# Prompt attention: the order of scores, weights' turns and value products on TensorE, and of exponents and copies on ScalarE

## The reference, cut to what matters

```python
o_c = p_c @ v_c                                   # compressed branch, 31 block keys
s_s = q @ k_s - slope * dist; p_s = softmax(s_s)  # "selected" branch (at 512 tokens all blocks are kept)
s_w = q @ k_w - slope * dist; p_w = softmax(s_w)  # window branch
o   = gate_c * o_c + gate_s * (p_s @ v_s) + gate_w * (p_w @ v_w)
```

## Time and profile before

| | |
|---|---|
| median of three runs | 1815.88 us |
| the profiled execution's own time | 1821.45 us |
| its span in the profile | 1819.7 us |
| share of the span busy: PE, DVE, ACT, POOL | 94%, 44%, 29%, 18% |
| the prompt attention stage, first maxima to last values | about 847.9 to 1030.6 us of the span |

### The profile page before, as it was taken

The page is one execution under the profiler, slowest core; times in us unless marked ns, Lnnn a source line. Parts: engine busy times, 40 slices in busy tenths (PEclk is TensorE's granted clock), DMA queues, the critical chain, the costliest instruction groups (busy, mean ns, idle before and its releaser), DMA issues. The chain is left out here.

```text
span 1819.7 us, 26521 instructions
## 1 busy us (share of the span) xinstructions
PE 1715.9 (94%) x9999; PEld 1139.1 (63%) x9999; DVE 794.3 (44%) x1937; ACT 520.8 (29%) x1247; POOL 336.4 (18%) x352
## 2 busy tenths in 40 slices
PE   8999999999999999998888899999998998999987
PEld 6587777877877878887665655575443443444332
DVE  1154664664664410566888552662222222222216
ACT  2234234233233221565667342111111110111110
POOL 0010211211111120222454550001111111111100
PEclk9999999999999999997999999989999999999998
DMA  8071221231232243452000673987999999999987
GB/s 246 1 225 49 71 75 49 60 86 49 60 77 56 48 113 110 118 163 65 1 1 1 232 229 133 386 331 296 400 419 421 420 420 420 421 419 420 419 344 318
DMA packets 168543, 371.70 MB, mean 204 GB/s; under 512 B 36903, under 2 KB 114719, under 8 KB 143584
## 3 DMA queue, kind: packets, MB, share of 16 engines
q1 hardware_dynamic: 148208, 308.69, 46.1%
q0 software_dynamic: 19728, 60.06, 9.4%
q10 hardware_dynamic: 480, 1.25, 0.2%
HBM read 337.75 MB, written 48.15 MB: 212 GB/s over the span
## 5 line engine op out<-in xcount | busy, mean ns | idle before, releaser
L860 PE MATMUL bank<-xT,arena 128*128 128x272 f32 x1440 | 368.1, 399 | 0.0
L860 PEld LDWEIGHTS bank<-xT,arena 128*128 128x128 f32 x1440 | 259.8, 190 | 62.3 <-issue 16.3
L2893 PE MATMUL bank<-arena,kvt 128*64 128x512 f32 (+1 forms) x816 | 258.5, 619 | 18.7 <-issue 17.8
L2893 PEld LDWEIGHTS bank<-arena,kvt 128*64 128x64 f32 (+1 forms) x816 | 88.1, 150 | 152.4 <-issue 152.4
L2990 PE MATMUL bank<-arena,kvt 128*64 128x512 f32 (+1 forms) x408 | 127.8, 598 | 2.3 <-issue 2.1
L3316 DVE SCALAR_TENSOR_TENSOR kvt<-kvt,arena,bank 128x256 f32<-128x256 f32 x37 | 17.8, 481 | 238.6 <-ACT kvt L3098 238.6
L1297 POOL TENSOR_TENSOR arena<-arena 128x512 f32<-128x512 f32 x40 | 46.4, 1160 | 381.3 <-DVE arena L1388 256.9
L2893 PE MATMUL bank<-xT,kvt 128*64 128x512 f32 (+1 forms) x208 | 95.4, 613 | 9.4 <-issue 9.4
L2730 POOL DMA_INDIRECT hT<-x_rows,rows_i x37 | 37.6, 1017 | 356.4 <-DVE rows_i L3251 334.3
L3098 ACT ACTIVATE kvt<-bank 128x256 f32<-128x256 f32 x37 | 14.2, 385 | 276.4 <-PE bank L2893 276.4
L3331 DVE COPY arena<-bank 128x512 f32<-128x512 f32 x37 | 25.6, 692 | 140.3 <-PE bank L2990 140.3
(11 more groups left out here) (519 smaller groups left out, 2971.8 us busy)
## 6 DMA issues: line engine op xcount, KB each, us to landing
arena<-in_w_exp_gate SPq DMA_DIRECT2D x51, 1024.0 KB, 21.4
arena<-in_w_exp_up SPq DMA_DIRECT2D x51, 1024.0 KB, 25.1
arena<-in_w_exp_down SPq DMA_DIRECT2D x51, 1024.0 KB, 23.5
arena<-in_w_in SPq DMA_DIRECT2D x48, 512.0 KB, 5.5
kvt<-in_w_exp_down SPq DMA_DIRECT2D x13, 1024.0 KB, 23.8
xT<-in_w_exp_gate SPq DMA_DIRECT2D x13, 1024.0 KB, 20.4
xT<-in_w_exp_up SPq DMA_DIRECT2D x13, 1024.0 KB, 25.1
y_rows<-arena SPq DMA_DIRECT2D x1, 12800.0 KB, 40.2
```

Of the source, the lines that this page charges most:

```text
L860: last = mm(banks[2 * (i % 2) + half][:, 0:HALF], wh[blk % RING][:, k, :], xT[:, k, half * HALF:(half + 1) * HALF], start=(k == 0), stop=( ...
L2893: last = mm(banks[2 + 4 * (t % 2)][cols, :], xgT[:, k, cols], ewgu[i % EBUF][:, :, k], start=(k == 0), stop=(k == KD - 1))
```

## The change

Three loops' orders change; no arithmetic is added or left out. On PE, `scores(i+3)` stands between the two parts of `turn_weights(i)` (the first part has t//2+1 fills: 1, 1, 2 and 2 for t = 0 to 3), except in rounds before 0 and in the four rounds with `cmp_scores`, where it still comes first. `values` is cut by branch into two halves, one in round 2u+2 and one in round 2u+3. On ACT, `exps(i+2)` no longer goes ahead of the copies of step i: its first branch follows the copies of the first part, its second branch the last copy.

```diff
--- before.py
+++ after.py
@@ -338,6 +338,12 @@
             if i >= 0:
                 P_FILL[i] = len(FILLS)
                 FILLS += ["a"] * (STEPS[i][0] + 1)
+
+        CMP_STEPS = [cmp_at(t) for t in range(4)]
+
+        def turned_first(i):
+
+            return STEPS[i][0] // 2 + 1
 
         def unit_gates(t, j):
 
@@ -1797,26 +1803,28 @@
                             last = tr(banks[4 + f % 2][:, (2 * br + g) * P:(2 * br + g + 1) * P], sc_p[i % 4][:, g, br, k * P:k * P + P], ident[:, :])
                     last.then_inc(tp_banked, 1)
 
-            def values(u):
+            def values(u, half):
 
                 t, j0 = STEPS[2 * u]
                 m = j0 // 2
-                if u >= 2:
-                    pe.wait_ge(mg_ready, u - 1)
-                last_fill = P_FILL[2 * u + 1] + t
-                pe.wait_ge(tp_saved_a, FILLS[0:last_fill + 1].count("a"))
                 out = banks[6 + u % 2]
-                for i in range(4):
-                    par, g = divmod(i, 2)
-                    mm(out[par * HD:par * HD + HD, g * P:g * P + P], vc_p[:, i], PcT[t % 2][:, m], start=(g == 0), stop=False)
-                for br in range(2):
+                if half == 0:
+                    if u >= 2:
+                        pe.wait_ge(mg_ready, u - 1)
+                    last_fill = P_FILL[2 * u + 1] + t
+                    pe.wait_ge(tp_saved_a, FILLS[0:last_fill + 1].count("a"))
+                    for i in range(4):
+                        par, g = divmod(i, 2)
+                        mm(out[par * HD:par * HD + HD, g * P:g * P + P], vc_p[:, i], PcT[t % 2][:, m], start=(g == 0), stop=False)
+                for br in (half,):
                     for k in range(t + 1):
                         for g in range(KVH):
                             c0 = (br + 1) * 256 + P + g * HD
                             for par in range(2):
                                 last = mm(out[par * HD:par * HD + HD, g * P:g * P + P], kvt[:, k, c0:c0 + HD],
                                           PT[u % 2][:, br, k, par, g * P:g * P + P], start=False, stop=(br == 1 and k == t and g == 1))
-                last.then_inc(pv_banked, 1)
+                if half == 1:
+                    last.then_inc(pv_banked, 1)
 
             halves = [slice(0, 64), slice(64, 128)]
 
@@ -1872,7 +1880,8 @@
                 last.then_inc(new_banked, 1)
 
             for i in range(-3, NSTEP + 1):
-                if i + 3 < NSTEP:
+                ahead = i < 0 or i in CMP_STEPS
+                if ahead:
                     scores(i + 3)
                 for t in range(4):
                     if cmp_at(t) == i:
@@ -1886,11 +1895,16 @@
                     turn_weights(i, 2, 4)
                     group_sums()
                 elif 0 <= i < NSTEP:
-                    turn_weights(i)
+                    turn_weights(i, 0, turned_first(i))
+                    if i + 3 < NSTEP and not ahead:
+                        scores(i + 3)
+                    turn_weights(i, turned_first(i))
                 if i == NSTEP - 2:
                     compressed_scores()
-                if i >= 2 and i % 2 == 0:
-                    values(i // 2 - 1)
+                if i >= 2:
+                    values(i // 2 - 1, i % 2)
+                if i == NSTEP:
+                    values(i // 2 - 1, 1)
 
 
             def turn_keys(x):
@@ -2064,20 +2078,24 @@
                 actv(gkv[0:HD, :, 0:NCMP_S], hsum[0:HD, :, 0:NCMP_S], ACT.Gelu_apprx_tanh).then_inc(gelu_done, 1)
             sc.wait_ge(cmpo_banked, NB + 1)
             actv(kcT_s[:, NB - 1], banks[6][:, 0:NCMP_S], ACT.Copy).then_inc(cmpk_saved, 1)
-            def exps(i):
+            def exps(i, br):
+
+                if i >= NSTEP:
+                    return
                 n = (STEPS[i][0] + 1) * P
                 a = ast[i % 4]
-                for br in range(2):
-                    for g in range(KVH):
-                        e = 2 * g + br
-                        sc.wait_ge(at_max, 4 * i + 2 * br + g + 1)
-                        last = actv(sc_p[i % 4][:, g, br, 0:n], sc_p[i % 4][:, g, br, 0:n], ACT.Exp, scale=-1.0, bias=a[:, e:e + 1],
-                                    accum_out=a[:, 4 + e:5 + e])
-                last.then_inc(at_exp, 1)
+                for g in range(KVH):
+                    e = 2 * g + br
+                    sc.wait_ge(at_max, 4 * i + 2 * br + g + 1)
+                    last = actv(sc_p[i % 4][:, g, br, 0:n], sc_p[i % 4][:, g, br, 0:n], ACT.Exp, scale=-1.0, bias=a[:, e:e + 1],
+                                accum_out=a[:, 4 + e:5 + e])
+                if br == 1:
+                    last.then_inc(at_exp, 1)
 
             for i in range(-2, NSTEP):
-                if i + 2 < NSTEP:
-                    exps(i + 2)
+                if i < 0:
+                    exps(i + 2, 0)
+                    exps(i + 2, 1)
                 for t in range(4):
                     if cmp_at(t) + 1 == i:
                         sc.wait_ge(cs_max, t + 1)
@@ -2105,6 +2123,9 @@
                         if u >= 2:
                             sc.wait_ge(pv_banked, u - 1)
                         actv(PT[u % 2][:, :, k, i % 2], banks[4 + f % 2][:, :].rearrange("p (r n) -> p r n", r=2), ACT.Copy).then_inc(tp_saved_a, 1)
+                        if k + 1 == turned_first(i):
+                            exps(i + 2, 0)
+                    exps(i + 2, 1)
 
             def save_keys(x):
```

## The result

The changed kernel takes 1859.46 us (median of four runs, 1857.03 to 1863.39) against 1816.82 us before in the same measurement: ratio 1.0241, 95% interval 1.0227 to 1.0256, 42.6 us slower. Measured again on another chip the ratio was 1.0241 (1.0223 to 1.0259). The forecast was slower by 27.6 us, so the sign and the mechanism held and the size was too small by a third. The measured time stands at the very end of the range that was given, 1829 to 1860.

A forecast was written before the change was run, and what follows sets the result against it. The prediction took the closed chain between DVE and PE, not a saturated engine, as the bound: 50.7 - 4.3 - 15.9 - 2.9 = +27.6 us, on the median 1815.9 + 27.6 = 1843.5 us, range 1829 to 1860.

The forecast's parts named there:

- The closed chain: Prompt attention: maxima, weights, first fills and scores form a loop without slack; at t = 3 wait 2.40, turn 6.9 us.
- The sum of the new waits: DVE's maxima behind 26 chains wait 50.7 us together; thirteen merges done in these waits take off 4.3 us.
- The low clock: Rival: PE stays at 1.2 GHz for steps 7 to 18, each chain 0.84 more, +10 us, 1853.5; chance 0.17.
- What the waits take in: On DVE, 4.3 us of merges, 15.9 of old waits for scores and 2.9 for POOL's bias go.
- The values in halves: PE's value products: no instruction added; in the tail up to +1.86 us, about as much the other way; booked at nothing.
- Exponents between copies: ACT's new order: most of PE's 7.4 us of waits for copies go, worth nothing to the sum.
- ACT's standing idle at the end: Idle 5.89 us as cache loads behind the last maximum start; expected again, worth up to -6 if missed.
- The rule of the most-contended engine: Skill page: improve the most-contended engine; by it the edit can't hurt and gains 7.4 us; the prediction argued against it.

The follow-up runs named there:

- e2: The kernel before with only the scores moved between the two parts of the turns; value products whole, ACT's order old: 1861.52 us, ratio 1.0246.
- e1: The changed kernel with the scores first again in every round; halved value products and ACT's new order stay: 1808.58 us, ratio 0.9962 to the kernel before.
- e3: The changed kernel with DVE's two calls exchanged, weights(i+1) before maxima(i+3) from round 0 on: 1827.05 us, ratio 1.0067 to the kernel before.
- e6: The changed kernel with eight unread matmuls more per round by the value products, to keep the clock up: 1859.25 us, ratio 1.0265 to the kernel before.
- e10: The changed kernel with six unread matmuls more in 16 of its rounds only: 1848.47 us, ratio 1.0226 to the kernel before.
- e8: The kernel before with ACT's new order of exponents and copies alone: 1809.06 us, ratio 0.9988.
- e7: The kernel before with the value products in two halves a step apart and nothing else: 1805.55 us, ratio 0.9968.
- e9: The kernel before with halved value products, but both halves of unit 14 in round 30, ahead of the group sums: 1800.65 us, ratio 0.9950.
- e4: The changed kernel with all fills of step i ahead of the scores of step i+3: 1887.46 us, ratio 1.0393 to the kernel before.

## Why the prediction was right in kind and too small

- **The closed chain.** Right. The order that gives it was named (weights, first fills, scores, maxima); its turn at t = 3 was put at 6.9 us and is 6.93, its wait at 2.40 and is 2.40. e2 shows that the scores' move alone makes the loss, e1 that without it there is none, e3 that exchanging two calls on DVE opens the chain though PE's order stays.
- **The sum of the new waits, 50.7 less 4.3 for merges, so 46.4 us.** This is the step that failed, a term that was mis-sized: it measured 54.0 (53.1 in the second profile), 7.6 of the 15.0 us by which the forecast fell short. The links were taken at full clock from step 7 on. In the profile after, the links of steps 7, 8, 9, 11, 17, 25 and 26 are at the lower level and 6.9 us longer in all (0.8, three times 1.0, 0.7, 1.6, 0.9); the mean granted clock from scores to maxima is 0.50 to 0.56 in each of them and 1.00 in all other steps from 10 on. And one fill costs 0.58 us up to the scores behind it where half of two fills, 0.51, was taken: 11 times 0.07, 0.8 us. Together 7.7, the whole of the difference (a wait of 0.3 at step 6 and one of 0.3 less at step 23 cancel). The low clock had stood there as a rival of its own, +10 us at steps 7 to 18 with 0.17; it came in part and also at t = 3, so it belonged into the middle of the forecast. That the long links are those at the low clock is read from the trace; that the time would fall by as much at full clock is not shown, since the two runs that raised the clock (e6, e10) paid for it elsewhere. The page TensorE: Matmul & The Clock Gate of the Trainium skill, section A second HAM failure mode, describes short idle times between groups of matmuls that make the clock swing; the trace agrees, with a granted clock of 0.87 in the mean of the stage instead of 0.93.
- **What the waits take in.** Right in the sum: the 2.9 us for POOL went to 0.3 (in e8 it does too, with PE's old order, so that need not be the change's doing), and no old wait was found beside the new ones. 54.0 - 18.9 leaves +35.1 of the stage's 38.6; of the other 3.5, booked at nothing, 1.1 is one merge waiting for its half product and 2.4 is DVE's own time (123.2 instead of 120.8 us). Of this, 1.4 us is the small product of 128x4 ahead of the weights (29 calls, 8.0 us instead of 6.6), the line that is long beside POOL's instructions in e3 too; the rest is open.
- **The values in halves, booked at nothing.** Wrong in two places. With the scores first they gain some 6 us (e7), which in the change can't be seen since the chain binds. And the stage's end, where +1.86 was set against a gain of the same size, costs 2.9 us (e9 takes it back): the price named was PE's half product; 1.2 us is DVE's queue behind the merge that waits for it, and the rest is open.
- **Exponents between copies, nothing.** Right: 0.9988 alone (e8).
- **What is left of the 15.0 us.** 7.6 (waits), 3.5 (the rest of the stage) and 2.9 (its end) make 14.0. The other 1.0 is scatter between executions: -1.4 behind the last maxima, +1.7 elsewhere, and 0.7 between the profiled executions and the medians.
- **ACT's standing idle at the end, 5.89 us.** ACT's wait there was 2.5 us in the changed kernel, and DVE stood idle for 4.65 us as before for 4.8. In the stretch from the last maxima to the last value product executions differ from 27 to 33 us without regard to the kernel (27.4 and 31.8 for the changed one).
- **The rule of the most-contended engine** (the Trainium skill, Perfetto Trace Analysis, section Identifying the Most-Contended Engine) did not hold here, as argued: PE and DVE do the same work, and the stage is 38.6 us longer.

## What to carry to other kernels

When engines run fixed queues, write down for a reordering, in order, what each instruction waits for, and look whether producer and consumer of two neighbouring steps have become one closed loop. A loop with a step of slack can hide its links, as in the round of the earlier trace rows; the same loop without slack adds every link to every step, even when all engines have idle time. If the new order makes TensorE wait in every round, price its links at the low clock too, not only at the old one. And read the size of an effect from the times: two profiles of kernels that run equally long (before and e8) had stages 4.8 us apart. And split an edit before judging it: here one part lost 2.5%, and another, hidden beneath it, wins 0.3 to 0.5%.

## What the runs showed that had not been expected

- The same program meets the low clock at other steps from execution to execution (of the links in chains, those of steps 7, 8, 9, 11, 17, 25 and 26 in one profile, 7, 9, 11, 20, 26 and 28 in another).
- Behind the last maxima, where the cache loads start, DVE stands idle in front of a merge with nothing in the profile that releases it: 4.8 us before, 4.65 in the changed kernel, 4.3, 5.7 and 4.6 in e1, e3 and e4, and in the other runs not at all. ACT's 5.89 us are put down to a DMA. In the changed kernel ACT has another such idle time of 8.8 us some 35 us behind the last maxima. The cause stays open.
- Four L2384 of 128x512 take 1.67 us alone and 2.37 with POOL's slopes beside them, and the L2381 of 128x4 ahead of them 0.16 and 0.59. With the calls exchanged (e3), where they run together in 26 of 32 rounds instead of 14, DVE's own time was 15 us longer.
